# Sample streams of a sparse-attention step: both halves of the next keys turned together behind the value products, and copied ahead of the normalization

## The reference, cut to what matters

```
keys = concatenate([past_k, k]); vals = concatenate([past_v, v])
logits = einsum('bqgjd,bqkgd->bqgjk', q_b, k_sel) * ATTN_SCALE + bias     # head size 64
logits = where(valid, logits, -inf)                                       # the 132 best keys of the index
probs = softmax(logits)
out = einsum('bqgjk,bqkgd->bqgjd', probs, v_sel);  out @ w_o
```

## Time and profile before

| what | us |
|---|---|
| median of three runs | 1809.35 |
| the profiled execution, its own time | 1810.91 |
| its span, first to last instruction | 1809.1 |
| TensorE busy (99% of the span) | 1786.6 |
| VectorE busy (73%) | 1313.3 |
| ScalarE busy (46%) | 825.8 |
| GpSimd busy (19%) | 348.8 |

### The profile page before, as it was taken

How to read it: one execution, slowest core, us unless ns; L and a number is a source line. 1 busy time by engine, 2 the same in 40 slices (tenths; PEclk the granted TensorE clock), 3 DMA queues, 4 the chain that set the end, 5 groups by cost and what they waited for, 6 DMA issues and landing times.

```text
span 1809.1 us, 35107 instructions
## 1 busy us (share of the span) xinstructions
PE 1786.6 (99%) x13025; PEld 1692.4 (94%) x13025; DVE 1313.3 (73%) x2450; ACT 825.8 (46%) x1477; POOL 348.8 (19%) x381
## 2 busy tenths in 40 slices
PE   8999999999999999999999999999999999999998
PEld 7887668999999999999999999998999999999998
DVE  5498976468576677978788888888535756758786
ACT  4223875334343433536545655456333434334353
POOL 0002663200000000123333343422020100000011
PEclk9999999999999999999999999999999999999999
DMA  6372144333343343233444334444323433334232
GB/s 162 75 121 66 61 135 136 97 87 88 90 95 91 77 111 77 69 79 108 140 138 141 105 122 124 145 139 153 119 81 97 97 94 82 100 82 97 77 84 76
DMA packets 326708, 186.27 MB, mean 103 GB/s; under 512 B 39536, under 2 KB 319184, under 8 KB 325552
## 3 DMA queue, kind: packets, MB, share of 16 engines
q1 hardware_dynamic: 307904, 173.49, 34.1%
q0 software_dynamic: 15840, 7.87, 3.5%
q10 hardware_dynamic: 2832, 3.15, 0.5%
HBM read 164.30 MB, written 19.99 MB: 102 GB/s over the span
## 4 chain that ended last, share of the span: by engine, by line
PE 81%; DVE 3%; ACT 1%; issue 1%; DVEq 0%; ACTq 0%
PE psum L1452 26%; PE psum L203 26%; PE psum L1517 19%; PE psum L621 1%; PE psum L625 1%; PE psum L572 1%; PE psum L585 1%; PE psum L2759 1%; PE psum L554 0%; PE psum L597 0%; PE psum L608 0%; DVE WL L195 0%; PE psum L2730 0%; PE psum L2743 0%; PE psum L566 0%
## 5 line engine op out<-in xcount | busy, mean ns | idle before, releaser
L203 PE MATMUL psum<-b2H,WH 128*128 128x320 f32 x896 | 213.7, 320 | 1.2 <-DVE b2L L1250 0.7
L1517 PE MATMUL psum<-HH,HT 128*128 128x320 f32 x680 | 210.4, 309 | 0.8 <-DVE xT L1731 0.4
L1517 PE MATMUL psum<-HL,HT 128*128 128x320 f32 x680 | 210.7, 310 | 0.0
L203 PE MATMUL psum<-b2H,WL 128*128 128x320 f32 x896 | 204.1, 309 | 0.0
L203 PE MATMUL psum<-b2L,WH 128*128 128x320 f32 x896 | 203.8, 308 | 0.0
L1452 PE MATMUL psum<-b2H,HT 128*128 128x320 f32 x816 | 186.1, 309 | 0.0
L1452 PE MATMUL psum<-b2L,HT 128*128 128x320 f32 x816 | 186.1, 309 | 0.0
L191 ACT ACTIVATE WH<-W 128x1024 fp32r<-128x1024 f32 x89 | 94.0, 1056 | 194.3 <-PE psum L203 180.8
L1517 PE MATMUL psum<-HH,LT 128*128 128x320 f32 x560 | 173.5, 310 | 0.0
L203 PEld LDWEIGHTS psum<-b2H,WH 128*128 128x128 f32 x896 | 146.3, 188 | 11.2 <-issue 8.4
L1452 PE MATMUL psum<-b2H,LT 128*128 128x320 f32 x672 | 153.1, 309 | 0.0
(11 more groups left out here) (437 smaller groups left out, 4203.2 us busy)
## 6 DMA issues: line engine op xcount, KB each, us to landing
W<-ssm_w_in SPq DMA_DIRECT2D x96, 256.0 KB, 3.1
RW<-mlp_w_up SPq DMA_DIRECT2D x64, 256.0 KB, 3.0
RWx<-mlp_w_up SPq DMA_DIRECT2D x64, 256.0 KB, 3.2
RW<-mlp_w_down SPq DMA_DIRECT2D x64, 256.0 KB, 3.1
RWx<-mlp_w_down SPq DMA_DIRECT2D x64, 256.0 KB, 3.2
bc<-scratch_acs SPq DMA_DIRECT2D x8, 1280.0 KB, 7.7
W<-attn_w_in SPq DMA_DIRECT2D x32, 256.0 KB, 3.8
prev<-state_ssm SPq DMA_DIRECT2D x16, 512.0 KB, 5.3
```

Of the source, the lines that this page charges most:

```text
L203: last = pe.matmul(psum[0:m, b.out + h, 0:TH], w[:, b.slot, k, 0:m], r[:, k, h * TH:(h + 1) * TH], start=(n == 0 and i == 0), stop=(n == K ...
L1517: last = pe.matmul(down_bank(g, i), w[:, k], x[:, DNB[i], k], start=(opens and k == 0 and c == 0), stop=(k == 3 and c == 2), skip_group_ch ...
```

## The change

`keys_bank` gives half 1 of every stream bank 5, and half 0 bank 6 (bank 4 for stream 0). In `sample_stream(b)` the second key half of b + 1 is no longer turned between the heads and the second probabilities; instead both halves of b + 2 are turned at the end of the stream, the second one waiting until the probabilities of stream b are copied out of bank 5 (`ptn`). The second probabilities of every stream but the last wait until both key halves of the next stream are copied (`ske`), since they share bank 5. On VectorE the key copy moves from behind the probability copy to between the second maximum and the normalization, now for stream b + 2.

```diff
     def keys_bank(b, a):
-        return 4 + a if b == 0 else 5 if (b, a) == (1, 1) else 6
+        return 5 if a else 6 if b else 4
...
                     wait(pe, ske, 2 * b)
                     if b_is(b, 1):
                         pe.wait_ge(oe, NU // 8)
-                elif b >= 1:
-                    pe.wait_ge(ske, 2 * b + (1 if b > 1 else 0))
+                elif b:
+                    pe.wait_ge(ptn, 2 * b - 2) if b > 1 else pe.wait_ge(ske, 2)
...
                 if a == 0:
                     pe.wait_ge(pte, NU + b)
-                elif g_is_first(b):
-                    pe.wait_ge(ske, 4)
+                elif not b_is(b, DB - 1):
+                    pe.wait_ge(ske, 2 * b + 4)
...
                 turn_probs(b, 0)
                 if not g_is_first(b):
                     turn_sample_heads(b - 1)
-                if not last and b:
-                    turn_keys(b + 1, 1 - s, i + s, 1)
                 turn_probs(b, 1)
                 weigh_sample(b, s, i, 0)
...
                 weigh_sample(b, s, i, 1)
                 if not last and not b_is(b, DB - 2):
                     turn_keys(b + 2, s, i + 1, 0)
+                    turn_keys(b + 2, s, i + 1, 1)
...
             def sample_step(b):
                 sample_turned(b)
                 last = b_is(b, DB - 1)
-                if not last and b:
-                    sample_keys(b + 1)
                 if not g_is_first(b):
                     sample_heads_lo(b - 1)
...
                 if not last:
                     sample_max(b + 1, 0)
                     sample_max(b + 1, 1)
+                if b + 2 < DB:
+                    sample_keys(b + 2)
                 sample_normalize(b)
```

## The result

| | before | changed |
|---|---|---|
| median, us | 1809.27 (9 runs) | 1813.86 (9 runs) |
| lowest and highest, us | 1808.83, 1810.82 | 1813.40, 1815.74 |
| span of the profiled execution, us | 1809.1 | 1812.1 |
| TensorE busy, us | 1786.6 | 1784.0 |

The changed kernel is slower by a factor of 1.0026, with a 95% interval of 1.0017 to 1.0034; the medians differ by 4.6 us. The forecast was 5.1 us and 1814.4.

What follows compares the result with a forecast made beforehand. TensorE is busy 99% of the span, and a closed chain of waits sets each sample stream's 5.65 us. The key copy ahead of the normalization adds 0.85 us in six streams, 5.1 us: 1814.4 us, range 1812.2 to 1816.0.

Steps and rivals of the forecast that it cites:

- What bounds the stage: Sample streams: a closed chain of waits, value products round to the next value products, sets the 5.65 us period; heads' slack 0.3.
- the 0.3 us put down to issue: TensorE's wait before the first value products; the profile names issue, the prediction reads ScalarE's tail copy ending 0.11 us ahead.
- The slot removed and the slot filled on TensorE: Second-half key transposes leave the place before the second probabilities and follow the first key half; each priced at 0.
- Banks and added waits: Second key half moves to bank 5; second probabilities wait for both key copies, expected done before 267.40; cost 0.
- VectorE's added copy: Key copy ahead of the normalization waits for transposes, starting it 1.15 us late; chain 6.50 against 5.65, 0.85 us per stream.
- How often: The copy precedes a normalization for keys of streams 2 to 7, so six streams: 6 x 0.85 = 5.1 us.
- After the stage: TensorE is busy from 320 to 500 us, so the delay is carried; at most 1.8 us in three waits could absorb it.
- The rule weighed: Trainium skill: a recurring gap can mean too little SBUF or PSUM, so the second bank would close it; trace names the exponential.
- The shared bank as the gap's cause: Rival: the idle 0.43 us per stream closes in six streams, 2.6 us faster, 1806.8; chance 0.05.
- Keys found ready: Rival: key transposes end by the second maximum, normalization only 0.65 late, 2.1 us slower in all, 1811.5; chance 0.07.
- Absorption: Rival: waits after the stage absorb 1.8 us, leaving 3.3 us slower, 1812.7; chance 0.06.
- The clock: Rival: TensorE's clock drops to 1.2 GHz in the slower streams, adding 31 us, 1845; chance 0.03.

Runs made afterwards that it cites:

- the tail first: ScalarE's copy of the first probability tail put ahead of the heads' high halves; ratio to the kernel before: 0.9999 with this edit on it, 1.0008 on the changed kernel.
- the copy behind the normalization: Changed kernel with VectorE's key copy moved behind the normalization, all else as changed; period 5.66 us, ratio 1.0002 to the kernel before.
- the copy in its old place: Changed kernel with VectorE's key copy back behind the next probability copy; period 6.62 us, ratio 1.0031 to the kernel before.
- split waits: Changed kernel, key copy behind normalization, first tail before heads, exponentials back to back, own semaphore for VectorE's key copies; period 5.47 us, ratio 0.9991 to the kernel before.
- a pad: Kernel before with extra 128x512 VectorE copies ahead of the normalization in streams 0 to 5; ratio 1.0010 with one, 1.0025 with two.
- the low heads moved: Split-waits order, with the prompt's low heads on VectorE taken one stream later, behind the next probability copy; period 6.23 us, ratio 1.0014 to the kernel before.
- the prompt's high halves early: Split-waits order, with ScalarE's high halves of the prompt ahead of its copy of the second probabilities; period 5.35 us, ratio 0.9995 to the kernel before.
- the last stream excepted: Prompt's high halves taken early on ScalarE in all streams but the last, on the split-waits order; period 5.35 us, median 1807.89, ratio 0.9993 to the kernel before.

## Why the prediction was right, by its steps

*What bounds the stage.* For the change, the chain read from the rows of before held: delaying one joint, the normalization, moved the period one for one beyond a slack of 0.28 (forecast 0.3), and taking the heads out of it in the changed kernel gave 0.55 us back. That the 0.3 us put down to issue were ScalarE's tail also holds: in the changed kernel the waits of a stream name it (0.5 us), and with the tail first the gap ahead of the value products shrinks from 0.33 to 0.22. What the prediction missed is that this chain is not alone. A second one of the same length ties ScalarE's copy of the second probabilities to the row maximum over the prompt's heads, so in the kernel before the row maximum does not wait for the logits, as the prediction has it: it follows VectorE's low halves. This did no harm to the forecast, since a delay beyond its slack lengthens the period whichever chain it lies on; a forecast of a gain from the first chain alone fails, as 5.55 did for the tail first.

*The slot removed and the slot filled on TensorE.* Priced at 0 and 0: right, by the copy behind the normalization, which has both and the old time.

*Banks and added waits.* Priced at 0 in the chosen place: right, though only there. With the copy in its old place the wait for bank 5 costs 0.97 a stream.

*VectorE's added copy.* The step that decided, right in mechanism and place. The sum was 6.50 and the trace shows 6.41; the joints that were too large are logits to first keys (1.88 in the rows of before, 1.83 now, since from the logits' first weights to the second value products it is 1.10 in place of 1.14) and copy to normalization (0.65 against 0.61).

*How often.* Six streams: right, but not six equal ones. The five periods from stream 1 on grew by 0.76 (6.41 less 5.65), 3.8 in all, the first by 0.73 (256.26 to 262.64, 6.38), and the last shrank by 0.07. The sum is 4.4 us where 6 x 0.85 = 5.1 stood; the median, at 4.6, came a little nearer to the forecast than the stage did, and that is within the scatter of the runs.

*After the stage.* Nothing was absorbed: the shift is 3.7 us at 358 us and 3.8 at 1800, and the waits for weights' low halves are again 1.8 us in three places, behind the same products of TensorE.

*The rule weighed.* The second bank alone did not close the repeating gap, so here the trace's releaser was the better guide than the rule of thumb. The kernel with split waits uses the bank and is shorter, but no run shows that it needs it.

*The rivals.* The shared bank as the gap's cause: refuted by the copy behind the normalization, 5.66 and not 5.2. Keys found ready: the copy waited 0.41 us. Absorption: not seen. The clock: 1.00 in the windows of the changed streams, so this rival falls too. At the very end the granted clock did fall in the profiled execution of before and not while TensorE worked in the changed one, which took 0.8 us off the difference of the spans.

## What to carry to other kernels

Before an operation is put ahead of another on a busy engine, look at what it waits for, not at how long it takes: this copy takes 0.69 us and would have cost nothing behind the normalization, but it waited for transposes and held a result that TensorE and, behind it, ScalarE were queued for. When a period is full of small waits, write down the closed chain from start to start; a pad of known length in one joint then tells its slack (0.28 us here) and whether it is on the chain. Look for a second closed chain before hoping for a gain: with two of one length, as here, shortening one leaves the period as it was, while a delay on either that exceeds its slack shows in full. The new bank alone brought nothing here; the shorter period came in a kernel that also split its wait from the others and reordered the work ahead.

## What the runs showed of the hardware that was not expected

VectorE's subtraction of two SBUF tiles (128x512, fp32) takes 0.69 us in all eight places of the kernel before. In the kernel with the low heads moved, six of the eight fell beside GpSimd's sum of 128x528: five took 1.18 to 1.22 us and one 1.81, while the sum kept its 1.30 to 1.33 us. The row of all eight:

```profile
L3207 DVE TENSOR_TENSOR b1L<-hF,b1H x8: 692/1185/1806, 261.2 to 300.8; 128x512 fp32r<-128x512 f32 x8
```

VectorE's copies from PSUM beside the same sum keep their 0.69 us (266.36 above, with GpSimd's sums from 265.65 and 267.13). The Trainium skill (GPSIMD Engine Reference, Specifications) says that GpSimd's SBUF interfaces are shared with VectorE and that they contend with VectorE instructions that have two SBUF inputs; the trace agrees. In all nine overlaps of three runs (six here, two with the prompt's high halves early, one with the last stream excepted) the sum had started first, and the subtraction ended 0.55 or 0.56 us after the sum did, whether it had started 0.07 us behind it or 0.97: it took as long as if it had waited for the sum's end. What happens when the subtraction starts first, no run shows. In the kernel before the subtraction stands where GpSimd waits for the next logits, a property of the order that no line of the code tells.
